# Two-layer diffusion step on one core: the order of the merged attention and projection steps, and softmax signals per head

## The reference, cut to what matters

```
z = h @ w_in                                   # 1024 -> 2304
conv_out = gate_b * short_conv(gate_c * xin)   # 512 channels
p = softmax(concat([q k_own / 8 (banded), q k_ctx / 8, sink]))[..., :-1]
o = p_own @ v_own + p_ctx @ v_ctx              # 8 query heads, 2 key heads
mix = concat([conv_out, o]) @ w_out
sh1, sc1, gt1, sh2, sc2, gt2 = silu(cond) @ mod_w + mod_b   # both layers
```

## Time and profile before

| | us |
|---|---|
| median of 3 runs | 3106.9 (3103.04 to 3114.9) |
| the profiled execution's own time | 3106.81 |
| its span in the profile | 3105.0 |
| units 0 to 17, about | 75 to 202 |
| units 18 to 53, with the 36 pairs | 202 to 635 |
| all that follows | 635 to 3105 |

### The profile page before, as it was taken

The page is one execution under the profiler, slowest core; times in us unless marked ns, Lnnn a source line. Parts: engine busy times, 40 slices in busy tenths (PEclk is TensorE's granted clock), DMA queues, the critical chain, the costliest instruction groups (busy, mean ns, idle before and its releaser), DMA issues. The chain is left out here.

```text
span 3105.0 us, 39476 instructions
## 1 busy us (share of the span) xinstructions
PE 2880.5 (93%) x14994; PEld 2493.3 (80%) x14994; DVE 1592.2 (51%) x2337; ACT 1359.0 (44%) x2157; POOL 159.4 (5%) x260
## 2 busy tenths in 40 slices
PE   5898878889999999999999998777899999999998
PEld 3666766667999999999989776776789999999997
DVE  6455645555454554554431355787454545445444
ACT  6344444454443443433331466554344434334333
POOL 0000000000000000000000003880000000000000
PEclk8999998999999999999999999888999999999999
DMA  6442122153444434444422442002534444444443
GB/s 238 142 151 79 58 82 68 55 155 103 123 125 125 147 122 123 148 124 127 123 70 62 136 129 88 7 1 91 181 109 122 123 128 142 128 128 143 128 128 109
DMA packets 309733, 355.12 MB, mean 114 GB/s; under 512 B 20086, under 2 KB 242748, under 8 KB 308572
## 3 DMA queue, kind: packets, MB, share of 16 engines
q1 hardware_dynamic: 300560, 331.52, 34.4%
q10 hardware_dynamic: 7020, 13.87, 1.3%
q0 software_dynamic: 2016, 7.86, 0.7%
HBM read 337.88 MB, written 15.34 MB: 114 GB/s over the span
## 5 line engine op out<-in xcount | busy, mean ns | idle before, releaser
L1260 DVE TENSOR_TENSOR p_lo<-p_raw,p_hi 128x1024 fp32r<-128x1024 f32 x507 | 619.6, 1223 | 743.7 <-ACT p_hi L724 743.2
L724 ACT ACTIVATE p_hi<-p_raw 128x1024 fp32r<-128x1024 f32 x507 | 533.1, 1052 | 569.2 <-DMA p_raw<-mlp_w 423.9
L2025 PE MATMUL ps<-hm_hi,p_hi 128*128 128x384 f32 x1536 | 515.7, 336 | 4.8 <-DVE hm_lo L1280 4.0
L2025 PE MATMUL ps<-hm_hi,p_lo 128*128 128x384 f32 x1536 | 515.8, 336 | 0.0
L2025 PE MATMUL ps<-hm_lo,p_hi 128*128 128x384 f32 x1536 | 514.4, 335 | 0.0
L1964 PE MATMUL ps<-p_hi,hid_hi 128*128 128x512 f32 x1152 | 363.5, 396 | 5.1 <-DVE p_lo L1260 5.1
L1964 PE MATMUL ps<-p_lo,hid_hi 128*128 128x512 f32 x1152 | 358.8, 393 | 0.0
L1964 PE MATMUL ps<-p_hi,hid_lo 128*128 128x512 f32 x1152 | 357.4, 392 | 0.0
L940 ACT ACTIVATE relu<-ps 128x384 f32<-128x384 f32 x192 | 94.5, 492 | 525.5 <-PE ps L2025 525.5
L1498 DVE TENSOR_TENSOR sqr<-relu 128x384 f32<-128x384 f32 x192 | 107.1, 558 | 377.8 <-ACT relu L940 377.8
L2025 PEld LDWEIGHTS ps<-hm_hi,p_hi 128*128 128x128 f32 x1536 | 288.4, 188 | 14.1 <-DVE hm_lo L1280 4.5
(11 more groups left out here) (238 smaller groups left out, 4093.6 us busy)
## 6 DMA issues: line engine op xcount, KB each, us to landing
p_raw<-mlp_w SPq DMA_DIRECT2D x384, 512.0 KB, 4.0
mod_p<-mod_w SPq DMA_DIRECT2D x80, 512.0 KB, 4.0
p_raw<-gla_w_in SPq DMA_DIRECT2D x56, 512.0 KB, 3.6
p_raw<-gla_w_out SPq DMA_DIRECT2D x24, 512.0 KB, 3.3
mod_w<-mod_w SPq DMA_DIRECT2D x8, 1024.0 KB, 13.0
p_raw<-ab_w_in SPq DMA_DIRECT2D x14, 512.0 KB, 5.4
p_raw<-ab_w_out SPq DMA_DIRECT2D x12, 512.0 KB, 3.6
p_raw<-ab_w_out SPq DMA_DIRECT2D x24, 256.0 KB, 3.9
```

Of the source, the lines that this page charges most:

```text
L724: nc.scalar.activation(p_hi[s][:, :, 0:width], p_raw[s][:, :, 0:width], ACT.Copy).then_inc(pan_hi, 1)
L1260: V.tensor_tensor(p_lo[s][:, :, 0:width], p_raw[s][:, :, 0:width], p_hi[s][:, :, 0:width].bitcast(F32), ALU.subtract).then_inc(pan_lo, 1)
L2025: mm = M.matmul(ps[:, b, 0:GN], w[s][:, c, :], x[:, c, :], start=(c == 0 and x is hi and w is p_hi), stop=(c == DC - 1 and w is p_lo))
```

## The change: what it does

Four edits, all in the merged stage:
1. Signals per head: `exps` does exponential and sink head by head and signals each; `normalise` does sum, reciprocal and multiplication head by head and signals each; `turn_weights` waits and signals per head; `turned_weights` copies a head as soon as it is turned.
2. ACT: `turned_weights` stands right behind `unit_take`, and the high parts of the next unit's blocks (`late_hi`) and the panel's high part behind it.
3. PE: the blocks of a unit (`late_mod`) come between the unit and `turn_weights`, no longer behind `turn_weights`.
4. The panel's high part is made at n = 0 of panel p for panel p+1 (before at n = 2 for p+2), its low part at n = 1. For pairs 0 to 3 (one block per head) the slot is given back by the next unit's first matmul, since the only transpose now carries `pt_ready`.

```
 # ACT, exps
                 for u in range(2):
                     act.wait_ge(s_max, 2 * p + u + 1)
-                    nc.scalar.activation(wide(out[u])[:, 0:n], s_bank(u)[:, 0:n],
-                                         ACT.Exp, bias=x[:, 1, u:u + 1], accum_out=x[:, 2, u:u + 1])
-                for u in range(2):
+                    nc.scalar.activation(wide(out[u])[:, 0:n], s_bank(u)[:, 0:n], ACT.Exp, bias=x[:, 1, u:u + 1],
+                                         accum_out=x[:, 2, u:u + 1])
                     head = p % 4 + 4 * u
-                    last = nc.scalar.activation(x[:, 3, u:u + 1], sink[:, head:head + 1], ACT.Exp, bias=x[:, 1, u:u + 1])
-                last.then_inc(s_exp, 1)
+                    nc.scalar.activation(x[:, 3, u:u + 1], sink[:, head:head + 1], ACT.Exp,
+                                         bias=x[:, 1, u:u + 1]).then_inc(s_exp, 1)
 # ACT, turned_weights
-                act.wait_ge(pt_ready, p + 1)
                 n = pair_width(p)
                 for u in range(2):
+                    act.wait_ge(pt_ready, 2 * p + u + 1)
                     last = nc.scalar.activation(...)
 # ACT, the loop over units
                 if pair is not None:
                     exps(pair)
-                for k in mods_after(u + 1):
-                    late_hi(k)
                 if pair:
                     output_take(pair - 1)
                 unit_take(u)
-                if n == 2 and p + 2 < IN_PANELS:
-                    panel_split_hi((p + 2) % 3, pieces=2 if 2 <= p + 2 < 6 else 1)
+                if pair is not None:
+                    turned_weights(pair)
+                for k in mods_after(u + 1):
+                    late_hi(k)
+                if n == 0 and 0 < p < IN_PANELS - 1:
+                    panel_split_hi((p + 1) % 3, pieces=2 if 2 <= p + 1 < 6 else 1)
 ...
-                if pair is not None:
-                    turned_weights(pair)
 # DVE, normalise
-                dve.wait_ge(s_exp, p + 1)
-                own(V.tensor_tensor(x[:, 2], x[:, 2], x[:, 3], ALU.add))
-                own(V.reciprocal(x[:, 0], x[:, 2]))
                 for u in range(2):
+                    dve.wait_ge(s_exp, 2 * p + u + 1)
+                    own(V.tensor_tensor(x[:, 2, u:u + 1], x[:, 2, u:u + 1], x[:, 3, u:u + 1], ALU.add))
+                    own(V.reciprocal(x[:, 0, u:u + 1], x[:, 2, u:u + 1]))
                     pr = wide(weights(p)[0][u])[:, 0:n]
-                    last = V.tensor_scalar(pr, pr, x[:, 0, u:u + 1], None, ALU.mult)
-                last.then_inc(s_norm, 1)
+                    V.tensor_scalar(pr, pr, x[:, 0, u:u + 1], None, ALU.mult).then_inc(s_norm, 1)
 # DVE, the loop over units
-                if n == 2 and p + 2 < IN_PANELS:
-                    split_lo((p + 2) % 3)
+                if n == 1 and 0 < p < IN_PANELS - 1:
+                    split_lo((p + 1) % 3)
 # PE, turn_weights
-                pe.wait_ge(s_norm, p + 1)
                 for u in range(2):
+                    pe.wait_ge(s_norm, 2 * p + u + 1)
                     for i in range(pair_width(p) // P):
                         last = turn(s_bank(u)[:, i * P:(i + 1) * P], weights(p)[0][u][:, i, :])
-                        if i == 0 and u == 0:
+                        if i == 0 and u == 0 and pair_width(p) > P:
                             used_before(last)
-                last.then_inc(pt_ready, 1)
+                    last.then_inc(pt_ready, 1)
 # PE, the loop over units
+                for k in mods_after(u):
+                    late_mod(k)
                 if pair is not None:
                     turn_weights(pair)
-                for k in mods_after(u):
-                    late_mod(k)
```

## The result

The changed kernel takes 3029.8 us (median of 4 runs, 3024.31 to 3035.83) against 3104.97 for the kernel before: a ratio of 0.9753 with a 95% interval of 0.9723 to 0.9782. The forecast was 3052, with a range from 3034 to 3082. The time fell as forecast, but by 75 us and not by 55, which is 4 us more than the range allowed.

The account below looks back on a forecast made before the run. PE was taken as the bound, losing time to ACT's late copies and a lower clock. Steps gained 65.7 us, less 2 for DVE and 8.5 for the clock: 55 us, from 3106.8 to 3052 us, range 3034 to 3082.

Parts of the forecast that it names:

- clock still lost in two-block steps: Units 18 to 53: a third of the sixteen two-block steps would still lose 1.7 us each to the clock, 8.5 us.
- length of the stage by its steps: Units 18 to 53: steps of 9.25, 10.25 and 11.25 us with none, one and two blocks; 65.7 us gained.
- units 0 to 17: Merged stage's first units: a gain of 0 to 3 us or a loss of up to 2, taken as 0.
- DVE late after the long convolution: Nines with the long convolution passes: maxima begin late on DVE, 0.5 us on each of four, 2 us taken off.
- everything behind the stage: The program after the merged stage: same instructions in the same order, so carried over unchanged.
- What bounds the kernel: Units 18 to 53: PE busiest, 362 of 433 us; 71 us idle and some 28 us of lower clock can be won.
- The circle: Merged stage: ACT's high part waits for PE's block behind turn_weights, delaying turned_weights and PE's scores; ACT waited 89.3 us.
- rival 1: Units 18 to 53: the clock gives nothing back, loss 27.9 us instead of 8.5; 3071 us, chance 0.17.
- rival 3: Merged stage: the wait only moves, ACT holding up exps, and 3.9 us return at turn_weights; 3104 us, chance 0.06.
- one-block steps become slower: Units 18 to 53: quiet one-block steps become 0.25 us slower, 10.25 us against 10.0.
- Rival 2: Units 18 to 53: DVE becomes the bound through extra sums, reciprocals and panel subtractions, 29 us; 3081 us, chance 0.10.
- The panels' move: Merged stage: panel p+1's high and low parts at n = 0 and n = 1, covered by a whole unit; cost nothing.

Follow-up runs that it names:

- run 1: The kernel before with only ACT's order changed (turned_weights right behind unit_take, the next unit's high parts behind it): 3073.6 us.
- run 2: The kernel before with only PE's order changed (blocks between the unit and turn_weights): 3074.3 us.
- Run 4: The changed kernel without the signals per head (one signal for both heads, as before), orders and panels as changed: 3041.7 us.
- run 7: The changed kernel with one extra ACT copy of each turned head into an unread buffer, ahead of the real copy: 3092.9 us.
- run 5: The changed kernel with the panels' high and low parts back at n = 2 for panel p+2, orders and signals as changed: 3034.8 us.
- run 6: The changed kernel without PE's new order (all blocks behind the transposes again), ACT's order, signals and panels as changed: 3028.8 us.
- run 3: The kernel before with only the signals per head added: 3094.6 us.
- run 9: The changed kernel with a unit's last block behind the transposes on PE and only the first of two ahead of them: 3007.1 us, ratio 0.9684.
- run 8: The changed kernel with one extra ACT copy for the first head and two for the second into an unread buffer: 3121.8 us.

## Why the prediction was wrong in its size

The predicted span was 3050.0 us (3105.0 - 55), the measured one 3029.6. The 20.4 us between them, term by term (0.2 is rounding):

| step of the prediction | put at | measured | difference |
|---|---|---|---|
| clock still lost in two-block steps | 8.5 | 0 (PEclk 1.00 in all 36) | 8.5 |
| length of the stage by its steps (9.25, 10.25, 11.25 us and the short ones) | 367.4 (433.1 - 65.7) | 361.0 | 6.4 |
| units 0 to 17 | 0 gained | 4.8 gained | 4.8 |
| DVE late after the long convolution | 2 | 0 | 2.0 |
| everything behind the stage | unchanged | 1.4 longer | -1.4 |

*What bounds the kernel* held. The circle from ACT's high part to PE's block and back through `turned_weights` is what runs 1 and 2 each break in part: run 1 took PE's waits at scores from 53.4 to 9.6 us and moved most of them to the transposes, run 2 cut the longest from 3.9 to 2.8. With the circle and DVE's wait for the panel both gone, 22.0 us of waits at scores are left and the lost clock is back. Rivals 1 and 3 fell with that: PEclk is 1.00, and ACT doesn't wait before `late_hi` in the stage.

*The step that failed* is the sizing of the terms, the clock's above all: a loss of 8.5 us was kept for the two-block steps, and none was measured. I had no row with a wait of about 1.15 us behind two blocks, and put a guess between none and all: a third, which for sixteen steps is 9.1 us (8.5 is five steps). Run 4 shows that there was room up to 1.4 us. The clock alone doesn't explain the miss: with 0 for it the forecast is 3043 us, still 13 too long, and the rest is the steps and units 0 to 17, mis-sized to the same side.

The rows that I took for the clock were also too few. In units 36 to 44 the one-block steps behind a wait of 1.1 us are at 1.00, and I wrote that no step with such a wait shows a loss. In units 27 to 35 and 45 to 53 of the kernel before all four such steps are at 0.85 and take 11.2 to 11.3 us, as the row at 309.46 above. By these rows an even larger loss could have been expected; the run showed none. Why a wait of 1.1 us was followed by a lower clock there and one of 1.4 us in run 4 never was stays open. A wait of 3.9 us stood one step ahead of all six, so it doesn't part them either.

I also read the loss as length times (1 - clock). That overstates it, at least in steps of the same work: in run 7 two of them differ by 12.80 - 11.26 = 1.54 us, where 0.87 would give 1.66, and in the kernel before by 11.17 - 10.01 = 1.16 us (units 28 and 37), where 0.85 would give 1.68.

*The steps* were right in build, each a little too long: a block costs 0.92 instead of 1.0, and from the first transpose to scores it takes 2.1 instead of 2.2. Both were read too high, and over 48 blocks and 36 steps that makes the 6.4 us. The order "one-block steps become slower" came out as said, 10.05 against 10.01.

*Units 0 to 17* I had put at 0 with a gain of up to 3. Runs 1, 4, 5 and 6, all with ACT's order, have 122.4 to 123.2 us there; runs 2 and 3, without it, 128.0 and 127.8. There is no attention pair in these units, so it is `unit_take` ahead of the high parts that brings 4 to 5 us, with a clock of 0.99 instead of 0.97. Through which wait of PE's was not taken apart.

*DVE late*: DVE is busy for 10.40 of 10.95 us in unit 43, the fullest step, and PE's waits show nothing of it: with both blocks ahead of the transposes the second head is normalised at 448.82, and PE turns it from about 449.07 (the first transpose starts at 448.55), so a quarter of a microsecond is in hand. Rival 2 fell here, but is what binds that step once a block goes behind them (run 9).

*The panels' move* I put at nothing, rightly as a cost; that without it edit 2 would push DVE's low part into the next step (rival 3's mechanism, by way of DVE) I had not seen. I had looked whether ACT's list had room for the panel's high part, and not who waits for it in the same step. Runs 1 and 5 show it, the latter at 12.6 us.

*The weights of the edits*: in the stage of 433.1 us, ACT's order alone brings 28 us, PE's alone 34, the signals alone 7, all four 72. The first two break the same circle, so their gains don't add. Beside the others PE's order brings nothing (run 6), the panels' move 13 (run 5), the signals 17 (run 4).

The rule of the Trainium skill named above, in TensorE: Matmul & The Clock Gate, "A second HAM failure mode: psum-queue depth-cycling", is borne out by runs 7 and 8, where idle times of 1.7 to 2.6 us in every step make the granted clock swing between its two levels. The changed kernel, with 0.84 us in each one-block step and 1.00 throughout the stage, isn't a case of it, nor is run 4 with 1.4 us.

## What to carry to other kernels

When an engine's list holds a wait for work that isn't due yet, move that item behind whatever another engine is waiting for; then look for who waits for the moved item within the same step, on a third engine, and move that too. Independent work on the bounding engine is cover, and it covers only what comes after it starts: one piece behind the producer's last instruction hides the consumer's copy, the rest ahead of it hides the preparation. Price the clock from steps that differ in nothing else, take every such step of the trace and not one neighbourhood, and where none has the wait in question, say that the part you put in the sum is a guess and keep both ends in the range.

## What the runs showed of the hardware that was not expected

How sharply the granted clock depends on short waits that come back in every step. With waits for ACT of 1.05 to 1.39 us in the steps of run 4 (10.6 us with one block) the clock stayed at 1.00 over 378 us. With 1.7 to 2.0 us in run 7 it was 0.93 over 423 us, with steps at 0.87 and others of the same work at 1.00; with 2.3 to 2.6 us in run 8 it was 0.90 over 454 us. So with some 0.6 us more of waiting in each step, in the same order of work, it goes from no loss to one of 19 us by estimate.

The length of a single wait doesn't settle it. In run 2 six full steps begin behind a wait of 2.8 us: three keep 1.00, and three lie at 0.78 or 0.87. In the kernel before, of the six full one-block steps behind a wait of 1.1 us, four lie at 0.85 and two at 1.00. What tells them apart no run here shows.
